# Up projection of a feed-forward layer: seven products of block sums in place of eight block products, for 8 of 22 tile pairs a layer

## The chip, the core and the metric

The kernel runs on one core of one Trainium2 chip. The metric is the device time of one execution in microseconds, the median of three runs. The core's engines work side by side: TensorE (PE in the profile; PEld is its weight load), VectorE (DVE), ScalarE (ACT), GpSimd (POOL) and SyncE (SP), whose queue issues the DMAs. They meet only in semaphores.

## The reference, cut to what matters

A model of two layers and one further block, on 512 tokens of width 1024, in float32. Each of the two layers ends with this feed-forward part (D_FF = 2816):

```python
h = rmsnorm(x, ffn_norm[l])
u = h @ ffn_w_up[l]                      # 1024 -> 2 * 2816
a, bv = u[..., :D_FF], u[..., D_FF:]
a = causal_dwconv(a, ffn_conv_w[l], ffn_conv_b[l])   # 3 taps along the tokens
x = x + (jax.nn.silu(a) * bv) @ ffn_w_down[l]
```

## The kernel before

Features lie on the 128 partitions, the 512 tokens along the free axis. Every float32 operand is kept as a high and a low part in the `F32R` type, and each product of blocks is three matmuls: high by high, high by low, low by high (`product`, lines 863 to 865). The high part of the weights is a ScalarE copy (`high`, line 1564), the low part a VectorE subtraction (`split_low`, line 1973); both work on a whole chunk of 2048 elements per partition (K = 8 blocks of 128 rows, 256 columns) or 1536 (K = 6). There are two slots of weights: chunk c lies in slot c % 2. SyncE loads chunk c once chunk c-2 is split (lines 1009 to 1018), ScalarE writes its high part once TensorE has finished chunk c-2, VectorE its low part after that.

The up projection has 22 tile pairs a layer. Pair f is one chunk: a gate tile and a value tile of 128 features each, 8 blocks by 3 matmuls of 512 columns, so 48 matmuls. The gate tile of an even f goes to PSUM bank 0, its value tile to bank 1, those of an odd f to banks 2 and 3. For each pair, in this order, VectorE scales the gate tile by the tokens' norm factor `rms_f` (line 2298), ScalarE takes the middle tap with the bias (line 1765), VectorE the other two taps (line 2303, twice), ScalarE the SiLU (line 1770), VectorE multiplies by `rms_f` again (line 2308) and by the value tile (line 2311), ScalarE and VectorE split the chunk that comes two pairs later, and then the hidden tile (lines 1775 and 2315). The 22 pairs are one loop of 11 iterations on VectorE, ScalarE and SyncE.

The down projection has 12 chunks in four groups of three (K = 8, 8, 6 blocks of the hidden axis); a group makes two output tiles of 512 tokens, one after the other within each chunk. VectorE adds each tile to `x_t` (line 2332), squares it and sums the squares (2334, 2338), writes the low part for the next stage (2341) and a second sum (2343). Its order is fixed: the split of two chunks, the group's two tiles, the split of the third chunk. After layer 0 the next layer begins with `raw_tiles` (lines 900 to 902), a norm statistic (803) and a gate product that needs VectorE's `kg` tile (2041). VectorE and ScalarE take their instructions strictly in program order, and almost every one is followed by a wait on its own semaphore. `upto` turns the count of an event into a threshold from loop registers.

## Time and profile before

| | |
|---|---|
| median of three runs | 2002.53 us (2002.37 to 2003.14) |
| the profiled execution | 2004.78 us, with a span of 2002.6 us from its first instruction to its last |
| TensorE busy | 1966.5 us, 98% of the span |
| VectorE busy | 1150.6 us, 57% |
| ScalarE busy | 826.2 us, 41% |
| mean granted TensorE clock | 0.995 |
| up projection of layer 0 | from about 263 to 506 us of the span |
| down projection of layer 0 | from about 506 to 626 us |

Busy time of TensorE counts from the first matmul of a queue to the modelled end of its last, and matmuls overlap: what one costs is read from the starts of two neighbours, not from its duration. Times in the rows below are microseconds from the start of the span, and means of groups are nanoseconds.

### The profile page before, as it was taken

Reading aid. Unit: us, or ns where it says so; the run is one execution under the profiler, and the core shown is the slowest. Engines: PE = TensorE matmul, PEld = TensorE weight load, DVE = VectorE, ACT = ScalarE, POOL = GpSimd, SP = SyncE. Lnnn points to the kernel's source line nnn. Section 1 sums busy time; section 2 is a strip of 40 time slices with the busy share of each in tenths; the row PEclk is TensorE's granted clock in tenths of the full one; section 3 lists DMA queues with packets and bytes.
Section 4 is the critical chain, followed back from the end, with each engine's and each line's share of the span. In section 5 each row is a group of like instructions: output and inputs, shape, how many; then the busy total and the mean of one; then the engine's idle time right before and its main releaser. Section 6 shows DMA issues by size and latency. Waiting matters only on the chain.

```text
span 2002.6 us, 29029 instructions
## 1 busy us (share of the span) xinstructions
PE 1966.5 (98%) x10962; PEld 1613.9 (81%) x10962; DVE 1150.6 (57%) x1382; ACT 826.2 (41%) x1211; POOL 25.9 (1%) x52
## 2 busy tenths in 40 slices
PE   7999999999999999999999999999999999999998
PEld 5897788888887897788888888987777766798888
DVE  6866765655445866766555445846664633443435
ACT  5445443333223345443333222334445555554444
POOL 2001000000000001000000000000000000000000
PEclk8999999999999999999999999999999999999999
DMA  6213133332224223133332223523332212232222
GB/s 192 75 47 105 43 105 105 84 105 85 94 95 120 69 55 106 43 105 96 93 104 85 95 95 80 183 73 99 89 110 68 63 53 64 84 115 76 92 87 85
DMA packets 239916, 181.26 MB, mean 91 GB/s; under 512 B 12842, under 2 KB 232232, under 8 KB 239422
## 3 DMA queue, kind: packets, MB, share of 16 engines
q1 hardware_dynamic: 237856, 177.37, 29.6%
q0 software_dynamic: 1520, 1.17, 0.3%
q10 hardware_dynamic: 430, 1.23, 0.3%
q8 instruction: 72, 1.18, 0.2%
q14 instruction: 38, 0.31, 0.1%
HBM read 168.21 MB, written 2.10 MB: 85 GB/s over the span
## 4 chain that ended last, share of the span: by engine, by line
PE 88%; DVE 6%; issue 2%; ACT 2%; DMA 1%; SPq 0%; DVEq 0%; ACTq 0%
PE ps L863 24%; PE ps L865 23%; PE ps L864 23%; PE ps L626 2%; PE ps L650 2%; PE ps L639 2%; DVE amat L2087 2%; PE ps L1285 1%; PE ps L1286 1%; PE ps L1287 1%; PE ps L506 1%; PE ps L475 1%; DMA w_raw<-in_w_in_dram 1%; PE ps L1169 1%; PE ps L495 1%
## 5 line engine op out<-in xcount | busy, mean ns | idle before, releaser
L863 PE MATMUL ps<-h_hi,w_hi 128*128 128x512 f32 x1376 | 553.8, 402 | 2.3 <-ACT qk L1557 2.0
L865 PE MATMUL ps<-h_hi,w_lo 128*128 128x512 f32 x1376 | 541.0, 393 | 0.0
L864 PE MATMUL ps<-h_lo,w_hi 128*128 128x512 f32 x1376 | 537.1, 390 | 0.0
L1973 DVE TENSOR_TENSOR w_lo<-w_raw,w_hi 128x2048 fp32r<-128x2048 f32 (+3 forms) x110 | 227.2, 2065 | 225.5 <-ACT w_hi L1564 218.0
L863 PEld LDWEIGHTS ps<-h_hi,w_hi 128*128 128x128 f32 x1376 | 259.4, 189 | 61.0 <-issue 7.4
L865 PEld LDWEIGHTS ps<-h_hi,w_lo 128*128 128x128 f32 x1376 | 259.2, 188 | 59.6
L864 PEld LDWEIGHTS ps<-h_lo,w_hi 128*128 128x128 f32 x1376 | 259.5, 189 | 56.0 <-issue 1.9
L1564 ACT ACTIVATE w_hi<-w_raw 128x2048 fp32r<-128x2048 f32 (+3 forms) x108 | 186.8, 1729 | 232.4 <-PE ps L865 211.9
L2362 DVE TENSOR_TENSOR w_lo<-w_raw,w_hi 128x1024 fp32r<-128x1024 f32 (+1 forms) x118 | 126.5, 1113 | 167.4 <-ACT w_hi L1816 166.7
L863 PE MATMUL ps<-w_hi,h_hi 128*128 128x256 f32 x544 | 152.4, 280 | 0.3 <-DVE h_lo L837 0.2
L864 PE MATMUL ps<-w_lo,h_hi 128*128 128x256 f32 x544 | 150.7, 277 | 0.0
L865 PE MATMUL ps<-w_hi,h_lo 128*128 128x256 f32 x544 | 150.7, 277 | 0.0
L863 PE MATMUL ps<-hid_hi,w_hi 128*128 128x512 f32 x352 | 138.7, 394 | 0.0
L865 PE MATMUL ps<-hid_hi,w_lo 128*128 128x512 f32 x352 | 138.0, 392 | 0.0
L864 PE MATMUL ps<-hid_lo,w_hi 128*128 128x512 f32 x352 | 136.6, 388 | 0.0
L1816 ACT ACTIVATE w_hi<-w_raw 128x1024 fp32r<-128x1024 f32 (+1 forms) x118 | 108.3, 965 | 4.1 <-issue 2.2
L863 PEld LDWEIGHTS ps<-w_hi,h_hi 128*128 128x128 f32 x544 | 102.3, 188 | 1.9 <-DVE h_lo L837 0.7
L1765 ACT ACTIVATE rms_a<-a_pad,g 128x512 f32<-128x512 f32 x44 | 35.9, 817 | 162.5 <-DVE a_pad L2298 162.5
L864 PEld LDWEIGHTS ps<-w_lo,h_hi 128*128 128x128 f32 x544 | 102.3, 188 | 0.1
L865 PEld LDWEIGHTS ps<-w_hi,h_lo 128*128 128x128 f32 x544 | 102.2, 188 | 0.0
L2303 DVE SCALAR_TENSOR_TENSOR rms_a<-a_pad,g,rms_a 128x512 f32<-128x512 f32 x88 | 66.2, 752 | 58.3 <-ACT rms_a L1765 51.7
L865 PEld LDWEIGHTS ps<-hid_hi,w_lo 128*128 128x128 f32 x352 | 66.1, 188 | 15.5
(390 smaller groups left out, 2767.6 us busy)
## 6 DMA issues: line engine op xcount, KB each, us to landing
w_raw<-in_ffn_w_up_dram SPq DMA_DIRECT2D x88, 512.0 KB, 4.6
w_raw<-in_w_in_dram SPq DMA_DIRECT2D x41, 1024.0 KB, 5.3
w_raw<-in_w_in_dram SPq DMA_DIRECT2D x32, 512.0 KB, 5.2
w_raw<-in_ffn_w_down_dram SPq DMA_DIRECT2D x32, 512.0 KB, 4.0
w_raw<-in_w_out_dram SPq DMA_DIRECT2D x12, 1024.0 KB, 5.6
w_raw<-in_ffn_w_down_dram SPq DMA_DIRECT2D x16, 384.0 KB, 3.4
swapped<-qk SPq DMA_DIRECT2D x96, 64.0 KB, 2.0
w_raw<-in_w_mem_kv_dram SPq DMA_DIRECT2D x4, 1024.0 KB, 5.8
```

Of the source, the lines that this page charges most:

```text
L626: ins = pe.matmul(ps[:, b, c:c + n], lhs, rhs, start=True, stop=True)
L639: ins = pe.transpose(ps[:, T_BANK + c // 512, c % 512:c % 512 + P], probs[:, e, c:c + P], ident)
L650: ins = pe.matmul(ps[64 * e:64 * e + 64, O_BANK, r * P:r * P + P], pairs[p].pv[e][k], probs_t[:, e, k * P:k * P + P], start=(k == 0), stop ...
L863: pe.matmul(dst, lh, rh, start=first and j == 0, stop=False)
L864: pe.matmul(dst, lh, rl, start=False, stop=False)
L865: ins = pe.matmul(dst, ll, rh, start=False, stop=last and j == len(order) - 1)
L1564: act.activation(w_hi[:, slot, 0:n], w_raw[:, slot, 0:n], ACT.Copy).then_inc(sem("w_high"), 1)
L1816: act.activation(w_hi[:, slot, q * n:q * n + n], w_raw[:, slot, q * n:q * n + n], ACT.Copy).then_inc(sem("w_high"), 1)
L1973: dve.tensor_tensor(w_lo[:, slot, 0:n], w_raw[:, slot, 0:n], w_hi[:, slot, 0:n].bitcast(F32), ALU.subtract).then_inc(sem("w_split"), 1)
L2087: dve.copy_predicated(amat[:].rearrange("p h t n -> p (h t) n"), levels[:, lv:lv + 1, :].to_broadcast([P, 4 * NT, P]), ps[:, MAIN:MAIN + 4 ...
L2303: dve.scalar_tensor_tensor(conv[:], a_pad[:, s, w:w + S], g[:, bass.ds(G_CONVW + w * KF + f, 1)], conv[:], ALU.mult, ALU.add).then_inc(sem ...
L2362: ins = dve.tensor_tensor(w_lo[:, slot, q * n:q * n + n], w_raw[:, slot, q * n:q * n + n], w_hi[:, slot, q * n:q * n + n].bitcast(F32), AL ...
```

## The change

In pairs 5, 7, ... 19 (8 of 22) the product of weights and tokens is taken as a 2 by 2 product of blocks: 4 of the 8 input blocks at a time by half of the tokens, gate rows and value rows. Seven products of block sums (Winograd's form of Strassen's scheme) take the place of eight: each is 4 blocks by 3 matmuls of 256 columns, so a pair has 84 matmuls of 256 columns in place of 48 of 512. The sums of tokens (`t_raw`) are made once a layer, during pairs 0 to 3. The sums of weights (`s_raw`) are made for each such pair by VectorE from the loaded chunk, and split like weights; one sum is written back into the chunk itself. VectorE puts the products together (`gate_fast`, `hidden_fast`). The hidden tiles stay unsplit in `hid` until pairs 20 and 21, where `hid_high` and `hid_low` split all 22. `rms_f` multiplies the down projection's output tiles in place of the SiLU's result. TensorE takes both output tiles of a down chunk block by block, so they are complete together. The counts of the new semaphores were added. The diff's core, its indentation taken back:

```diff
@@ constants and buffers @@
+FAST_FROM, FAST_TO = 5, 19
+FAST = (FAST_TO - FAST_FROM) // 2 + 1
-hid_hi, hid_lo = at("hid_hi", 0, [P, KF, S], F32R), at("hid_lo", 44, [P, KF, S], F32R)
+hid = at("hid", 0, [P, KF, S])
+hid_hi, hid_lo = at("hid_hi", 44, [P, KF, S], F32R), at("hid_lo", 0, [P, KF, S], F32R)
+y_blk = at("y_blk", 44, [P, 768])
+sums, u2 = at("sums", 40, [P, 3, 256]), at("u2", 43, [P, 256])
+s_raw, s_lo, s_hi = at("s_raw", 44, [P, 3, 4, P]), at("s_lo", 44, [P, 3, 4, P], F32R), at("s_hi", 50, [P, 3, 4, P], F32R)
+t_hi = at("t_hi", 56, [P, 4, 4, 256], F32R)
+t_raw, t_lo = at("t_raw", 72, [P, 4, 4, 256]), at("t_lo", 72, [P, 4, 4, 256], F32R)
...
@@ TensorE @@
+def fast_pair(i, n):
+    f = 2 * i + 1
+    t = T_UP + 2 * f
+    own = (slice(256, 512), slice(0, 256))
+    wh, wl = slot_view(w_hi, 1, KD), slot_view(w_lo, 1, KD)
+    block = lambda k0, row: lambda k: (wh[:, k0 + k, row * P:row * P + P], wl[:, k0 + k, row * P:row * P + P])
+    summed = lambda j: lambda k: (s_hi[:, j, k, :], s_lo[:, j, k, :])
+    tokens_ = lambda k0, c: lambda k: (h_hi[:, k0 + k, own[c]], h_lo[:, k0 + k, own[c]])
+    mixed_t = lambda j: lambda k: (t_hi[:, j, k, :], t_lo[:, j, k, :])
+    part = lambda bank, c: ps[:, bank, c * 256:c * 256 + 256]
+    split_ready(C_UP + f)
+    pe.wait_ge(sem("tile_copied"), upto(pe, "tile_copied", t - 2))
+    product(pe, part(5, 0), block(0, 1), tokens_(0, 0), range(4)).then_inc(sem("p1_done"), 1)
+    product(pe, part(2, 1), block(4, 1), tokens_(4, 0), range(4))
+    pe.wait_ge(sem("t_split"), upto(pe, "t_split", 4))
+    product(pe, part(4, 0), block(0, 0), mixed_t(2), range(4))
+    product(pe, part(4, 1), block(4, 0), mixed_t(3), range(4))
+    pe.wait_ge(sem("s_split"), upto(pe, "s_split", n + 1))
+    product(pe, part(3, 0), summed(1), mixed_t(1), range(4))
+    product(pe, part(3, 1), summed(0), mixed_t(0), range(4)).then_inc(sem("tile_done"), 1)
+    product(pe, part(2, 0), summed(2), tokens_(4, 1), range(4)).then_inc(sem("tile_done"), 1)
 up_tile(0, 0, 0)
 sum_stat(pe, 8)
-with pe.Fori(0, KF // 2 - 1) as i:
-    up_tile(i, 0, 1)
-    up_tile(i, 1, 0)
-    up_tile(i, 1, 1)
-    up_tile(i + 1, 0, 0)
-up_tile(KF // 2 - 1, 0, 1)
-up_tile(KF // 2 - 1, 1, 0)
-up_tile(KF // 2 - 1, 1, 1)
+up_tile(0, 0, 1)
+for f in range(1, FAST_FROM - 1):
+    for half in range(2):
+        up_tile(f // 2, f % 2, half)
+with pe.Fori(0, FAST) as n:
+    i = n + FAST_FROM // 2
+    for half in range(2):
+        up_tile(i, 0, half)
+    fast_pair(i, n)
+for f in range(FAST_TO + 1, KF):
+    for half in range(2):
+        up_tile(f // 2, f % 2, half)
 count["tile_done"] = 2 * C_DOWN
...
+            wh, wl = slot_view(w_hi, j % 2, K), slot_view(w_lo, j % 2, K)
+            if part == 0:
+                pe.wait_ge(sem("tile_copied"), upto(pe, "tile_copied", T_DOWN + 4 * i + 2 * q - 2))
+            for k in range(K):
+                pe.wait_ge(sem("hid_lo"), upto(pe, "hid_lo", 8 * part + k + 1))
+                for half in range(2):
+                    dst, c = ps[:, 2 * q + half, :], slice(half * P, half * P + P)
+                    h = 8 * part + k
+                    pe.matmul(dst, wh[:, k, c], hid_hi[:, h, :], start=h == 0, stop=False)
+                    pe.matmul(dst, wh[:, k, c], hid_lo[:, h, :], start=False, stop=False)
+                    ins = pe.matmul(dst, wl[:, k, c], hid_hi[:, h, :], start=False, stop=h == KF - 1)
+                    if k == K - 1:
+                        ins.then_inc(sem("tile_done"), tick("tile_done"))
@@ ScalarE @@
+def conv_start(f, slot):
+    act.wait_ge(sem("tile_copied"), upto(act, "tile_copied", T_UP + 2 * f + 1))
+    act.activation(conv[:], a_pad[:, slot, 2:S + 2], ACT.Identity,
+                   scale=g[:, bass.ds(G_CONVW + 2 * KF + f, 1)],
+                   bias=g[:, bass.ds(G_CONVB + f, 1)]).then_inc(sem("conv0"), 1)
+    act.wait_ge(sem("conv0"), upto(act, "conv0", f + 1))
+def conv_silu(f):
+    act.wait_ge(sem("conv"), upto(act, "conv", 2 * f + 2))
+    act.activation(conv[:], conv[:], ACT.Silu).then_inc(sem("silu"), 1)
+    act.wait_ge(sem("silu"), upto(act, "silu", f + 1))
+def up_high(f, slot):
+    act.wait_ge(sem("tile_done"), upto(act, "tile_done", T_UP + 2 * f + 2))
+    high(C_UP + f + 2, slot, KD, sum(dmas[slot][:C_UP // 2]) + f - slot + 4)
+def sums_high(f, n):
+    act.wait_ge(sem("s_sum"), upto(act, "s_sum", 4 * n + 4))
+    up_high(f, 1)
+    act.activation(s_hi[:], s_raw[:], ACT.Copy).then_inc(sem("s_high"), 1)
+def block_copies(j):
+    act.wait_ge(sem("t_sum"), upto(act, "t_sum", 4 * j))
+    act.activation(y_blk[:, 0:512], x_t[:, j], ACT.Copy, scale=col(G_FFN + j, 1))
+    act.activation(y_blk[:, 512:768], x_t[:, 4 + j, 256:512], ACT.Copy, scale=col(G_FFN + 4 + j, 1)).then_inc(
+        sem("y_blk"), tick("y_blk"))
+def block_high(j):
+    act.wait_ge(sem("t_sum"), upto(act, "t_sum", 4 * j + 4))
+    act.activation(t_hi[:, :, j, :], t_raw[:, :, j, :], ACT.Copy).then_inc(sem("t_high"), tick("t_high"))
+def hid_high(k):
+    act.wait_ge(sem("tile_copied"), upto(act, "tile_copied", T_UP + 2 * k + 2))
+    act.activation(hid_hi[:, k], hid[:, k], ACT.Copy).then_inc(sem("hid_hi"), 1)
+for f in range(FAST_FROM - 1):
+    conv_start(f, f % 2)
+    block_copies(f)
+    conv_silu(f)
+    if f + 2 < FAST_FROM:
+        up_high(f, f % 2)
+    else:
+        sums_high(f, 0)
+    block_high(f)
+def fast_act(n):
+    f = 2 * n + FAST_FROM - 1
+    conv_start(f, 0)
+    act.wait_ge(sem("p1_done"), upto(act, "p1_done", n + 1))
+    act.activation(sums[:, 2], ps[:, 5, 0:256], ACT.Copy).then_inc(sem("p1_kept"), 1)
+    up_high(f, 0)
+    conv_silu(f)
+    conv_start(f + 1, 1)
+    conv_silu(f + 1)
+with act.Fori(0, FAST - 1) as n:
+    fast_act(n)
+    sums_high(2 * n + FAST_FROM, n + 1)
+fast_act(FAST - 1)
+up_high(FAST_TO, 1)
+for f in (FAST_TO + 1, FAST_TO + 2):
+    conv_start(f, f % 2)
+    conv_silu(f)
+    up_high(f, f % 2)
+    for k in range(8 * (f - FAST_TO - 1), 8 * (f - FAST_TO)):
+        hid_high(k)
+for k in range(16, KF):
+    hid_high(k)
@@ VectorE @@
+def gate_fast(f, n):
+    pair = ps[:, 3:5, :].rearrange("p b n -> p (b n)")
+    dve.wait_ge(sem("tile_done"), upto(dve, "tile_done", T_UP + 2 * f + 1))
+    dve.wait_ge(sem("p1_kept"), upto(dve, "p1_kept", n + 1))
+    dve.tensor_tensor(u2[:], sums[:, 2], ps[:, 3, 0:256], ALU.add).then_inc(sem("fast_sum"), 1)
+    dve.wait_ge(sem("fast_sum"), upto(dve, "fast_sum", 3 * n + 1))
+    dve.tensor_tensor(sums[:, 0:2], u2[:].unsqueeze(1).to_broadcast([P, 2, 256]), halves(pair[:, 256:768]),
+                      ALU.add).then_inc(sem("fast_sum"), 1)
+    dve.wait_ge(sem("fast_sum"), upto(dve, "fast_sum", 3 * n + 2))
+    dve.tensor_tensor(halves(a_pad[:, 1, 2:S + 2]), sums[:, 0:2], halves(pair[:, 512:1024]),
+                      ALU.add).then_inc(sem("fast_sum"), 1)
+    dve.wait_ge(sem("fast_sum"), upto(dve, "fast_sum", 3 * n + 3))
+    dve.scalar_tensor_tensor(a_pad[:, 1, 2:S + 2], a_pad[:, 1, 2:S + 2], -1.0, rms_f[:], ALU.mult,
+                             ALU.mult).then_inc(sem("tile_copied"), 1)
+def conv_taps(f, slot):
+    dve.wait_ge(sem("conv0"), upto(dve, "conv0", f + 1))
+    for w in (1, 0):
+        dve.scalar_tensor_tensor(conv[:], a_pad[:, slot, w:w + S], g[:, bass.ds(G_CONVW + w * KF + f, 1)], conv[:],
+                                 ALU.mult, ALU.add).then_inc(sem("conv"), 1)
+        dve.wait_ge(sem("conv"), upto(dve, "conv", 2 * f + 2 - w))
+def hidden(f, src):
+    dve.wait_ge(sem("silu"), upto(dve, "silu", f + 1))
+    dve.wait_ge(sem("tile_done"), upto(dve, "tile_done", T_UP + 2 * f + 2))
+    dve.tensor_tensor(hid[:, bass.ds(f, 1), :].rearrange("p a n -> p (a n)"), src, conv[:],
+                      ALU.mult).then_inc(sem("tile_copied"), 1)
+    dve.wait_ge(sem("tile_copied"), upto(dve, "tile_copied", T_UP + 2 * f + 2))
+def hidden_fast(f, n):
+    dst = hid[:, bass.ds(f, 1), :].rearrange("p a n -> p (a n)")
+    dve.wait_ge(sem("tile_done"), upto(dve, "tile_done", T_UP + 2 * f + 2))
+    dve.tensor_tensor(halves(dst), sums[:, 0:3:2], halves(ps[:, 2, :]), ALU.add).then_inc(sem("c1_joined"), 1)
+    dve.wait_ge(sem("c1_joined"), upto(dve, "c1_joined", n + 1))
+    dve.wait_ge(sem("silu"), upto(dve, "silu", f + 1))
+    dve.tensor_tensor(dst, dst, conv[:], ALU.mult).then_inc(sem("tile_copied"), 1)
+    dve.wait_ge(sem("tile_copied"), upto(dve, "tile_copied", T_UP + 2 * f + 2))
+def plain(slot):
+    return ps[:, 2 * slot + 1, :]
+def weight_sums(f, n, first):
+    if first:
+        dve.wait_ge(sem("tile_done"), upto(dve, "tile_done", T_UP + 2 * f + 2))
+        dve.wait_ge(sem("w_loaded1"), upto(dve, "w_loaded1", 16 * (sum(n_dma[1::2][:C_UP // 2]) + f + 3)))
+        dve.tensor_tensor(s_raw[:, 0], raw1[:, 0:4, 0:P], raw1[:, 4:8, 0:P], ALU.add).then_inc(sem("s_sum"), 1)
+        dve.wait_ge(sem("s_sum"), upto(dve, "s_sum", 4 * n + 1))
+        dve.tensor_tensor(s_raw[:, 1], s_raw[:, 0], raw1[:, 0:4, P:2 * P], ALU.add).then_inc(sem("s_sum"), 1)
+        dve.wait_ge(sem("s_sum"), upto(dve, "s_sum", 4 * n + 2))
+    else:
+        dve.tensor_tensor(s_raw[:, 2], s_raw[:, 1], raw1[:, 4:8, P:2 * P], ALU.add).then_inc(sem("s_sum"), 1)
+        dve.tensor_tensor(raw1[:, 0:4, 0:P], raw1[:, 0:4, 0:P], raw1[:, 0:4, P:2 * P], ALU.add).then_inc(sem("s_sum"), 1)
+        dve.wait_ge(sem("s_sum"), upto(dve, "s_sum", 4 * n + 4))
+def sums_low(f, n):
+    split_low(C_UP + f + 2, 1, KD)
+    dve.wait_ge(sem("s_high"), upto(dve, "s_high", n + 1))
+    dve.tensor_tensor(s_lo[:], s_raw[:], s_hi[:].bitcast(F32), ALU.subtract).then_inc(sem("s_split"), 1)
+def block_sums(j):
+    y1, y2, y4 = y_blk[:, 256:512], y_blk[:, 0:256], y_blk[:, 512:768]
+    t = lambda q: t_raw[:, q, j, :]
+    dve.wait_ge(sem("y_blk"), upto(dve, "y_blk", j + 1))
+    dve.tensor_tensor(t(0), y1, y2, ALU.subtract).then_inc(sem("t_sum"), 1)
+    dve.scalar_tensor_tensor(t(2), x_t[:, 4 + j, 0:256], col(G_FFN + 4 + j, 1), y2, ALU.mult,
+                             ALU.subtract).then_inc(sem("t_sum"), 1)
+    dve.wait_ge(sem("t_sum"), upto(dve, "t_sum", 4 * j + 2))
+    dve.scalar_tensor_tensor(t(1), t(2), -1.0, y1, ALU.mult, ALU.subtract).then_inc(sem("t_sum"), 1)
+    dve.wait_ge(sem("t_sum"), upto(dve, "t_sum", 4 * j + 3))
+    dve.scalar_tensor_tensor(t(3), t(1), -1.0, y4, ALU.mult, ALU.subtract).then_inc(sem("t_sum"), 1)
+    dve.wait_ge(sem("t_sum"), upto(dve, "t_sum", 4 * j + 4))
+def block_low(j):
+    dve.wait_ge(sem("t_high"), upto(dve, "t_high", j + 1))
+    dve.tensor_tensor(t_lo[:, :, j, :], t_raw[:, :, j, :], t_hi[:, :, j, :].bitcast(F32), ALU.subtract).then_inc(
+        sem("t_split"), 1)
+def hid_low(k):
+    dve.wait_ge(sem("hid_hi"), upto(dve, "hid_hi", k + 1))
+    dve.tensor_tensor(hid_lo[:, k], hid[:, k], hid_hi[:, k].bitcast(F32), ALU.subtract).then_inc(sem("hid_lo"), 1)
+dve.wait_ge(sem("rms"), upto(dve, "rms", 4))
+dve.wait_ge(sem("pad"), upto(dve, "pad", 1))
+for f in range(FAST_FROM - 1):
+    gate_tile(f, f % 2)
+    conv_taps(f, f % 2)
+    hidden(f, plain(f % 2))
+    if f + 2 < FAST_FROM:
+        split_low(C_UP + f + 2, f % 2, KD)
+        block_sums(f)
+    else:
+        block_sums(f)
+        weight_sums(f, 0, True)
+        weight_sums(f, 0, False)
+        sums_low(f, 0)
+    block_low(f)
+def fast_even(n):
+    f = 2 * n + FAST_FROM - 1
+    gate_tile(f, 0)
+    conv_taps(f, 0)
+    split_low(C_UP + f + 2, 0, KD)
+    hidden(f, plain(0))
+with dve.Fori(0, FAST - 1) as n:
+    fast_even(n)
+    f = 2 * n + FAST_FROM
+    gate_fast(f, n)
+    weight_sums(f, n + 1, True)
+    conv_taps(f, 1)
+    weight_sums(f, n + 1, False)
+    hidden_fast(f, n)
+    sums_low(f, n + 1)
+fast_even(FAST - 1)
+gate_fast(FAST_TO, FAST - 1)
+conv_taps(FAST_TO, 1)
+hidden_fast(FAST_TO, FAST - 1)
+split_low(C_UP + FAST_TO + 2, 1, KD)
+for f in (FAST_TO + 1, FAST_TO + 2):
+    gate_tile(f, f % 2)
+    conv_taps(f, f % 2)
+    hidden(f, plain(f % 2))
+    split_low(C_UP + f + 2, f % 2, KD)
+    for k in range(8 * (f - FAST_TO - 1), 8 * (f - FAST_TO)):
+        hid_low(k)
+for k in range(16, KF):
+    hid_low(k)
...
-            dve.tensor_tensor(one(x_t), one(x_t), ps[:, j, :], ALU.add).then_inc(sem("tile_copied"), 1)
+            dve.tensor_tensor(b_sb[:], ps[:, j, :], rms_f[:], ALU.mult).then_inc(sem("down_scaled"), 1)
+            dve.wait_ge(sem("down_scaled"), upto(dve, "down_scaled", m + 1))
+            dve.tensor_tensor(one(x_t), one(x_t), b_sb[:], ALU.add).then_inc(sem("tile_copied"), 1)
```

## Rows read from the trace of the kernel before

**Rows 1.** Busy in a stretch: PE, PEld, DVE, ACT, POOL (instructions), clock, DMA
```profile
400.00:500.00 100.00, 100.00 (x439) 82.04 (x438) 58.97 (x65) 34.95 (x36) 0.00 (x0) 1.00 0.33 95
```

**Rows 2.** Timeline, TensorE: start, duration; every twelfth matmul, three places
```profile
400.10 0.39 PE L863 MATMUL ps<-h_hi,w_hi 128*128 128x512 f32 x1
402.85 0.39 PE L863 MATMUL ps<-h_hi,w_hi 128*128 128x512 f32 x1
...
1952.56 0.28 PE L1540 MATMUL ps<-w_hi,h_hi 128*128 128x256 f32 x1
1953.97 0.28 PE L1540 MATMUL ps<-w_hi,h_hi 128*128 128x256 f32 x1
...
1963.26 0.28 PE L1540 MATMUL ps<-w_hi,h_hi 128*128 128x256 f32 x1
1964.62 0.28 PE L863 MATMUL ps<-w_hi,h_hi 128*128 128x256 f32 x1
```

**Rows 3.** Timeline of VectorE, one pair
```profile
401.17 0.69 DVE L2298 TENSOR_TENSOR a_pad<-ps,rms_f 128x512 f32<-128x512 f32 x1 [0.61 <-PE ps L865]
403.01 0.75 DVE L2303 SCALAR_TENSOR_TENSOR rms_a<-a_pad,g,rms_a 128x512 f32<-128x512 f32 x1 [1.15 <-ACT rms_a L1765]
403.92 0.75 DVE L2303 SCALAR_TENSOR_TENSOR rms_a<-a_pad,g,rms_a 128x512 f32<-128x512 f32 x1 [0.15 <-DVE rms_a L2303]
408.75 2.29 DVE L1973 TENSOR_TENSOR w_lo<-w_raw,w_hi 128x2048 fp32r<-128x2048 f32 x1 [1.58 <-ACT w_hi L1564]
410.96 0.68 DVE L2315 TENSOR_TENSOR hid_lo<-b_sb,hid_hi 128x512 f32 x1
```

**Rows 4.** Timeline of ScalarE, the same pair
```profile
402.05 0.82 ACT L1765 ACTIVATE rms_a<-a_pad,g 128x512 f32<-128x512 f32 x1 [3.99 <-DVE a_pad L2298]
404.76 0.63 ACT L1770 ACTIVATE rms_a<-rms_a 128x512 f32<-128x512 f32 x1 [1.90 <-DVE rms_a L2303]
406.64 1.92 ACT L1564 ACTIVATE w_hi<-w_raw 128x2048 fp32r<-128x2048 f32 x1 [1.25 <-PE ps L865]
```

**Rows 5.** Groups by line and shape, VectorE and ScalarE, other widths
```profile
L2535 DVE TENSOR_TENSOR y_tok<-ps,g_row 128x256 f32<-128x256 f32 x16 | 6.8, 424 | 15.1 <-ACT sq L1947 14.9
L1973 DVE TENSOR_TENSOR w_lo<-w_raw,w_hi 128x1536 fp32r<-128x1536 f32 x8 | 14.1, 1759 | 48.3 <-ACT w_hi L1564 48.3
...
L1614 ACT ACTIVATE sig_r<-tm 128x1024 f32<-128x1024 f32 x2 | 2.1, 1061 | 0.1
L1947 ACT ACTIVATE sq<-ps 128x256 f32<-128x256 f32 x16 | 6.1, 382 | 21.9 <-PE ps L865 18.8 <-PE ps L1542 3.0
```

**Rows 6.** Timelines of VectorE and ScalarE, start of the up projection
```profile
270.65 0.69 DVE L2298 TENSOR_TENSOR a_pad<-ps,rms_f 128x512 f32<-128x512 f32 x1 [1.23 <-ACT rms_f L810]
291.33 0.69 DVE L2298 TENSOR_TENSOR a_pad<-ps,rms_f 128x512 f32<-128x512 f32 x1 [0.64 <-PE ps L865]
...
272.10 0.82 ACT L1765 ACTIVATE rms_a<-a_pad,g 128x512 f32<-128x512 f32 x1
275.80 1.92 ACT L1564 ACTIVATE w_hi<-w_raw 128x2048 fp32r<-128x2048 f32 x1 [0.33 <-ACT rms_a L1770]
```

**Rows 7.** Timeline of VectorE, second tile of a down group, next split
```profile
596.30 0.69 DVE L2332 TENSOR_TENSOR x_t<-x_t,ps 128x512 f32 x1 [0.29 <-DVE rms_f L2343]
600.43 2.29 DVE L1973 TENSOR_TENSOR w_lo<-w_raw,w_hi 128x2048 fp32r<-128x2048 f32 x1 [0.27 <-DVE rms_f L2343]
```

**Rows 8.** Timelines of VectorE and TensorE, layer 0 to layer 1
```profile
630.79 2.29 DVE L1973 TENSOR_TENSOR w_lo<-w_raw,w_hi 128x2048 fp32r<-128x2048 f32 x1 [0.27 <-DVE rms_f L2343]
640.69 0.69 DVE L2041 TENSOR_TENSOR kg<-ps,rms_a 80x512 f32<-80x512 f32 x1 [0.60 <-DVE cq L2041]
...
637.95 0.48 PE L863 MATMUL ps<-h_hi,w_hi 128*128 128x512 f32 x1
```

**Rows 9.** A long wait of TensorE's; busy times in a stretch behind it
```profile
PE ps L639 <- ACT prob_bt L697: 4.4, 4, 2.0
...
1622.00:1624.00 2.00, 2.00 (x6) 1.52 (x6) 0.65 (x1) 1.56 (x4) 0.00 (x0) 0.50 0.56 165
```

67 lines of the change are left out of this document (11 added, 56 removed).

## The prediction, blind

> **What bounds the kernel now.** I read the page's busy shares first (in the table of times), then the windows, then the timeline of each engine over one pair. In the up projection TensorE never rests: 100 us busy of 100, at full clock, beside 59 us of VectorE and 35 us of ScalarE [rows 1]. It starts one matmul of 512 columns every 0.229 us (twelve in 2.75 us) [rows 2], so a pair is 48 x 0.229 = 10.99 us and two pairs 21.97. Nothing but TensorE's work sets the time there. VectorE waits for it before each gate tile (0.61 us in the bracket) and for ScalarE in between, 0.15 to 1.6 us at a time [rows 3]. So the question is what a fast pair saves TensorE, and whether the two other engines, which take their instructions in order, can follow.
>
> **TensorE's part.** A fast pair is 7 products x 4 blocks x 3 = 84 matmuls of 256 columns. Twelve of them take 1.41 us in one place and 1.36 in another [rows 2]: 0.1175 or 0.1133 each, so 9.87 or 9.52 us a pair. I take 0.116, as the first place lies directly behind a stream of 512 columns, as here: 9.74 us, 1.24 less than 10.99. Sixteen such pairs would give 19.9 us, if nothing else came to bound them (17.9 to 23.5).
>
> **The loop of an even and a fast pair.** TensorE would need 10.99 + 9.74 = 20.7 us. Now follow VectorE and ScalarE through one iteration, from `u2` to the next `u2`. Durations: VectorE 0.69 us for 512 elements, 0.75 with a scalar from memory, 2.29 for a chunk [rows 3]; ScalarE 0.82, 0.63, 1.92 [rows 4]; VectorE 0.42 for 256 and 1.76 for 1536, ScalarE 0.38 for 256 [rows 5]. Hand-overs: VectorE to ScalarE 0.19 (401.86 to 402.05), ScalarE's chunk to VectorE's 0.19 (408.56 to 408.75), tap to tap 0.15, and an overlap of 0.08 where nothing is waited for (411.04 to 410.96) [rows 3, 4]. A wait on the engine's own last result is not shown alone. Its bounds are -0.08, the overlap, and 0.33, SiLU to chunk, where two more thresholds stand behind it [rows 6]. I take 0.04, and 0.3 where more thresholds follow, as a tile of the down projection has five instructions of 3.57 us in 4.13, of which the last gap is 0.27 [rows 7].
> - The gate put together, 0.42 + 3 x 0.69 + three gaps: 2.6 us. First two weight sums: 3.9. Gap and two taps, 0.29 + 1.65: 5.9. Second two sums: 7.2.
> - ScalarE's high part, 0.38 + 1.92: 9.5. VectorE's low part, 0.19 + 2.29: 12.0. Here the chunk of the next fast pair is ready.
> - `s_lo` and the next gate tile, 1.76 + 0.69 less overlaps: 14.3. ScalarE's middle tap, its copy of the first product and the even chunk's high part, 0.19 + 0.82 + 0.17 + 0.38 + 1.84: 17.7. Low part and hidden tile: 20.8. Gap: 21.1.
>
> ScalarE's high part must wait for the second weight sums, which write into the chunk, and these stand behind the taps; the hidden tile stands behind the low part. So this is one chain of 21.1 us, and it is longer than TensorE's 20.7. The saving is 21.97 - 21.1 = 0.9 us an iteration, not 1.24. The Trainium skill speaks against this ("VectorE: DVE Perf Modes", The DRAIN you can't avoid): a semaphore after each instruction costs nothing extra, which would leave the chain below TensorE's time and the whole at the 1996 us of the first rival; the rows' 0.15 behind an own wait, against an overlap without one, do not bear it out. Whether a matmul of 256 columns costs 0.113 or 0.1175 us changes nothing, as 20.9 is below 21.1 too.
>
> **Before the loop.** In pairs 0 to 3 VectorE and ScalarE make and split the sums of tokens. One pair's chain: gate 0.69, 0.19, middle tap 0.82, 0.14, taps 1.6, 0.09, SiLU 0.63, 0.33, high 1.92, 0.19, low 2.29, four sums of 256 elements 1.7, then ScalarE's high part of 1024 elements 1.06 [rows 5] and VectorE's low part 1.2 (between 0.69 and 1.76) with gaps of 0.1: 13.0 us, against 10.99 of TensorE. The removed `rms_f` product lies beside ScalarE's chunk and gives nothing. The first gate tile starts at 270.65 and its middle tap 0.57 us late (272.10), so that of pair 3 starts at 270.65 + 0.57 + 3 x 13.0 = 310.2 [rows 6]. From there to the end of chunk 5's split are gate to SiLU 4.2, hidden 0.8, token sums 1.7, four weight sums 2.8, high 2.2, low 2.5: 324.4. TensorE ends pair 4 two and a half pairs after the gate tile of 291.33: 318.7 [rows 6]. **TensorE waits 5.7 us before the first fast pair.** The next one comes 22.3 us later (s_lo, t_lo and an even pair stand before its `u2`), then six at 21.1: 148.9 us, against 7 x 21.97 = 153.8 before: 4.9 less. The last fast pair is 1.24 shorter. The up projection nets 5.7 - 4.9 - 1.2 = -0.4 us a layer.
>
> A wait this long may drop the clock: behind a wait of up to 2.0 us (at 1618 us) a stretch ran at 0.50, the lower level of 1.2 GHz [rows 9]. That would stretch fast pair 5 by 1.7 us, but 20.7 + 1.7 is just what the chain needs there (22.3), so I count nothing; at most 2 us a layer.
>
> **Behind the loop.** In pairs 20 and 21 the splits of 16 hidden tiles are put between: 8 x 0.61 us on ScalarE, 8 x 0.65 on VectorE each. Pair 21's work then ends about 11 us behind its tiles, but TensorE is on the first down chunk, which needs hidden tiles 0 to 7 alone; tile 8's low part comes about 0.3 us late. Each down tile has one product more, 0.73 us, and both tiles of a group end together, so VectorE's work on the first is no longer beside the second. It starts 0.6 us before the group ends, takes 2 x (4.13 + 0.73) = 9.7, then a split of 2.29: ready 11.4 us behind the group, where TensorE wants it after 10.99 [rows 3, 7]. That is 0.5 us, three times a layer. The down projection: +1.8 us a layer. Before, that split began 4.13 us behind the second tile's start [rows 7] and had room.
>
> **Layer 0 to 1.** The split of 630.79 ends at 633.1 and `kg` at 641.38, just as TensorE, which begins its tile at 637.95 and needs `kg` after 15 matmuls, comes to 641.4 [rows 8]. With the split ending at 637.4 and the same 4.35 us of small work behind it (0.5 to 1 us a piece), `kg` is ready at 643.9: +2.5 us, once. Behind layer 1 nothing waits for it.
>
> **Sum.** 2 x (-0.4 + 1.8) + 2.5 = +5.3; with the rounding of the terms +5. The sum is made against the profiled execution, whose 2004.78 us are its span of 2002.6 and 2.2 around it; it stands 2.2 above the median of 2002.53. I carry the difference over to the median: 2007.5 us.
>
> **Rivals.** A measurement of this kernel can tell 0.2%, 4.0 us, from no change.
> - *The waits are nearly free* (faster). If own waits cost as little as the overlap of 0.08 suggests, the chain loses some 0.9 us and falls below 20.7: TensorE sets the loop again. Then a layer is +4.1 before the loop, -8.2 in it, -1.2, +0.9: -4.4; twice, with +2.2: 1996. For: the 0.04 within a tile. Against: 0.15 and 0.27 in loops of the same kind [rows 3, 7]. It decides at 0.4 us of gaps an iteration. By the Trainium skill's sentence above it would be so. Chance 0.22.
> - *Between the two*, 1998.5 to 2003. Chance 0.10.
> - *Longer gaps* (slower). The new thresholds are computed from loop registers, up to four to a step. With 0.3 at each own wait the chain is 21.9, no gain in the loop; 7.4 us are waited for before it and 3.5 lost behind it: (7.4 + 0.6 - 1.2 + 3.5) x 2 + 3.5 = +24. Half of that excess is 2017. Chance 0.13.
> - *The forecast*, 2003 to 2014, chance 0.55, of which 0.25 lies within 0.2%.
>
> That the change doesn't do what it says, I exclude but for the cadence, which is bounded above. Sum: faster 0.22, same 0.35, slower 0.43. The range of 1995 to 2017 leaves a tenth out on either side; the forecast's own is 2003 to 2014.
>
> **What would show it.** Right: TensorE idle some 6 us before the first matmul of 256 columns on `ps` in either layer, released by `w_lo`; idle 0.2 to 0.6 us before each later fast pair, released by `w_lo` too; fast pairs 21.0 to 21.2 us apart; 0.5 us before each down group's second chunk; the `kg` tile 2 to 3 us late. Wrong: fast pairs 20.7 apart without idle time (the first rival), or 21.9 (the third); a first wait under 3 us, which would mean that the chain of pairs 0 to 3 is below 12.3.

## The result, and the profile after

The changed kernel takes 2007.78 us (median of seven runs, 2006.70 to 2011.83), the kernel before 2003.14 us beside it (seven runs, 2002.37 to 2006.12): a ratio of 1.0025, 95% interval 1.0015 to 1.0034. So it is 4.6 us slower, on a forecast of 2007.5. The profiled execution has a span of 2004.8 us, that of the kernel before 2002.6. A fast pair below is one of the eight that are made from block sums, an even pair one of the ordinary ones between them.

TensorE does less work and the kernel is not faster. The page's busy shares and clock:

```profile
PE 1956.7 (98%) x11538; PEld 1630.8 (81%) x11538; DVE 1257.8 (63%) x1538; ACT 867.6 (43%) x1267; POOL 25.9 (1%) x52
...
PEclk8999999999999999999999999999999999999999
```

VectorE has 107 us more work than before, ScalarE 41. The waits of TensorE (line, releaser: us in total, times, longest) have three rows of more than a microsecond that the kernel before has not:

```profile
PE ps L872 <- DVE w_lo L2068: 7.8, 2, 3.9
...
PE ps L1396 <- DVE w_lo L2068: 2.0, 6, 0.4
...
PE ps L1190 <- DVE kg L2136: 1.7, 1, 1.7
```

The first stands before the first fast pair of each layer (line 872 is `product`), the second before the second chunk of three of the four down groups, the third at the start of layer 1. TensorE's timeline over the first fast pair's start, the fast pair after it, and the start of the next, then the first fast pair of layer 1:

```profile
321.60 0.38 PE L872 MATMUL ps<-h_hi,w_hi 128*128 128x256 f32 x1 [3.92 <-DVE w_lo L2068]
...
344.21 0.28 PE L872 MATMUL ps<-h_hi,w_hi 128*128 128x256 f32 x1
...
345.62 0.28 PE L872 MATMUL ps<-h_hi,w_hi 128*128 128x256 f32 x1
...
351.29 0.28 PE L872 MATMUL ps<-t_hi,s_hi 128*128 128x256 f32 x1
...
352.73 0.28 PE L872 MATMUL ps<-h_hi,s_hi 128*128 128x256 f32 x1
...
354.17 0.39 PE L872 MATMUL ps<-h_hi,w_hi 128*128 128x512 f32 x1
...
365.17 0.28 PE L872 MATMUL ps<-h_hi,w_hi 128*128 128x256 f32 x1
...
928.74 0.58 PE L872 MATMUL ps<-h_hi,w_hi 128*128 128x256 f32 x1 [3.92 <-DVE w_lo L2068]
```

In the loop TensorE waits for nothing. A fast pair takes 354.17 - 344.21 = 9.96 us, an even pair 11.00, so fast pairs are 20.96 us apart against 21.97 for two pairs before. Twelve matmuls of the first product take 1.41 us, 0.1175 each; twelve of a product with summed weights take 1.44, 0.120 each. And the first fast pair is followed by the next only after 22.61 us, 1.65 more than the others, and in layer 1 only after 23.42 us (928.74 to 952.16), 2.46 more. Busy times in two stretches (window: its length, then PE, PEld, DVE, ACT and POOL busy with their instructions, granted clock, DMA share, GB/s) show why:

```profile
321.60:326.40 4.80, 4.80 (x27) 4.80 (x28) 3.63 (x4) 1.25 (x3) 0.00 (x0) 0.65 0.76 213
...
644.50:651.20 6.70, 6.70 (x17) 5.15 (x17) 5.22 (x6) 3.88 (x7) 0.00 (x0) 0.54 0.61 194
```

Behind the wait of 3.92 us much of the stretch ran at the lower level of the clock, 1.2 GHz, with matmuls of 256 columns 0.213 us apart (in layer 1 the first 24 of them). The same happened behind the wait for `kg`, where matmuls of 512 columns are 0.425 us apart until 650.8. TensorE's timeline there:

```profile
637.05 0.48 PE L872 MATMUL ps<-h_hi,w_hi 128*128 128x512 f32 x1
...
643.25 1.52 PE L1190 MATMUL ps<-kg,wg 16*128 16x512 f32 x2 [1.73 <-DVE kg L2136]
...
660.73 1.17 PE L1151 MATMUL ps<-lin 32*128 32x128 f32 x32
```

And in the kernel before:

```profile
642.36 1.12 PE L1181 MATMUL ps<-kg,wg 16*128 16x512 f32 x2
656.67 1.17 PE L1142 MATMUL ps<-lin 32*128 32x128 f32 x32
```

The kernel before takes 656.67 - 637.95 = 18.72 us for this stretch (its first matmul is in [rows 8]), the changed one 660.73 - 637.05 = 23.68: 4.96 us more, of which 1.79 stand ahead of the `kg` matmul and 3.17 behind it. I call it the `kg` stretch. The feed-forward parts that the change touches are even: from the up projection's first value tile to the end of the layer, layer 0 takes 369.39 us against 369.42, layer 1 369.75 against 369.79. Within each, gains and costs cancel. TensorE's matmuls at the first value tile and at the start of the down projection, layer 0, of the kernel before and then of the changed one:

```profile
268.53 0.80 PE L863 MATMUL ps<-h_hi,w_hi 128*128 128x512 f32 x1
...
505.16 0.39 PE L863 MATMUL ps<-hid_hi,w_hi 128*128 128x512 f32 x1
...
267.66 0.80 PE L872 MATMUL ps<-h_hi,w_hi 128*128 128x512 f32 x1
...
501.79 0.39 PE L1396 MATMUL ps<-hid_hi,w_hi 128*128 128x512 f32 x1
```

So the up projection takes 234.13 us instead of 236.63 (234.74 in layer 1), 2.50 and 1.89 less, with the waits before the first fast pairs and the slow clock behind them included. The down projection takes 122.47 instead of 120.62, 1.85 more in either layer, and what follows it 0.62 more in layer 0.

So the parts that the change touches lose 4.96 - 0.03 - 0.04 = 4.9 us, all of it in one stretch of 24 us. The two profiled executions are only 2.2 us apart, because the changed kernel's was 2.7 us faster in parts that are the same in both kernels: 0.9 ahead of the up projection, 0.3 in layer 1 ahead of its up projection, and 1.5 behind layer 1, where the kernel before ran a stretch at half clock [rows 9] and the changed one did not. That is chance, so the 4.6 us between the medians and the 4.9 us of the traces agree no better than within a few microseconds.

### The profile page after: what moved, and what is told of

Its sections match the earlier page's. It is cut to its first block, busy times and chain, and to the rows that moved or that the text cites. A ratio compares the mean times of both kernels' runs of the same rounds, so it can differ in the third digit from the quotient of the medians.

```text
span 2004.8 us, 30593 instructions
## 1 busy us (share of the span) xinstructions
PE 1956.7 (98%) x11538; PEld 1630.8 (81%) x11538; DVE 1257.8 (63%) x1538; ACT 867.6 (43%) x1267; POOL 25.9 (1%) x52
## 4 chain that ended last, share of the span: by engine, by line
PE 79%; DVE 12%; ACT 4%; issue 4%; DVEq 0%; DMA 0%; ACTq 0%; SPq 0%
PE ps L872 18%; PE ps L874 17%; PE ps L873 17%; PE ps L1396 3%; PE ps L1397 3%; PE ps L1398 3%; PE ps L635 2%; PE ps L659 2%; PE ps L648 2%; DVE w_lo L2068 2%; DVE amat L2182 2%; PE ps L1294 1%; PE ps L1295 1%; PE ps L1296 1%; PE ps L515 1%
## 5 line engine op out<-in xcount | busy, mean ns | idle before, releaser
L872 PE MATMUL ps<-h_hi,w_hi 128*128 128x512 f32 (+1 forms) x1248 | 489.6, 392 | 10.2 <-DVE w_lo L2068 7.8
L874 PE MATMUL ps<-h_hi,w_lo 128*128 128x512 f32 (+1 forms) x1248 | 478.9, 384 | 0.0
L873 PE MATMUL ps<-h_lo,w_hi 128*128 128x512 f32 (+1 forms) x1248 | 476.8, 382 | 0.0
L872 PEld LDWEIGHTS ps<-h_hi,w_hi 128*128 128x128 f32 x1248 | 237.2, 190 | 63.6 <-issue 17.5
L874 PEld LDWEIGHTS ps<-h_hi,w_lo 128*128 128x128 f32 x1248 | 237.2, 190 | 46.7
L873 PEld LDWEIGHTS ps<-h_lo,w_hi 128*128 128x128 f32 x1248 | 237.4, 190 | 45.1 <-issue 1.9
L1396 PEld LDWEIGHTS ps<-hid_hi,w_hi 128*128 128x128 f32 x352 | 66.1, 188 | 19.4 <-DVE w_lo L2068 3.0
```

The lines of the kernel that those rows point to most:

```text
L872: pe.matmul(dst, lh, rh, start=first and j == 0, stop=False)
L873: pe.matmul(dst, lh, rl, start=False, stop=False)
L874: ins = pe.matmul(dst, ll, rh, start=False, stop=last and j == len(order) - 1)
L1396: pe.matmul(dst, wh[:, k, c], hid_hi[:, h, :], start=h == 0, stop=False)
```

## The experiments

Times are medians; ratios are against the kernel before, run beside them. Its own medians were 2004.36 us beside sums_early, down_halves, amat_late and both, 2004.42 beside plain, plain_halves, extra_op and s_from_w, 2005.73 beside both_swapped and 2004.19 beside the last two, and 2003.14 beside the changed kernel. So differences of a microsecond or two between kernels of different groups are not read from the times but from the traces.

| run | us | ratio, 95% interval |
|---|---|---|
| sums_early | 1993.41 | 0.9945 (0.9931 to 0.9959) |
| down_halves | 2000.50 | 0.9977 (0.9966 to 0.9987) |
| amat_late | 2002.27 | 0.9991 (0.9982 to 1.0000) |
| both | 1987.45 | 0.9910 (0.9895 to 0.9925) |
| plain | 2011.72 | 1.0036 (1.0023 to 1.0050) |
| plain_halves | 2002.95 | 0.9994 (0.9985 to 1.0003) |
| extra_op | 2020.93 | one run |
| s_from_w | 2006.35 | one run |
| both_swapped | 1987.76 | 0.9915 (0.9902 to 0.9929) |
| extra_reordered | 2011.78 | one run |
| both_reordered | 1983.98 | 0.9898 (0.9882 to 0.9915) |

**Which wait costs what.** In the changed kernel, VectorE's timeline over pair 1, one of the four in which the token sums are made:

```profile
282.84 0.68 DVE L2391 TENSOR_TENSOR a_pad<-ps,rms_f 128x512 f32<-128x512 f32 x1
...
288.90 2.29 DVE L2068 TENSOR_TENSOR w_lo<-w_raw,w_hi 128x2048 fp32r<-128x2048 f32 x1 [1.41 <-ACT w_hi L1607]
...
294.04 1.23 DVE L2468 TENSOR_TENSOR t_lo<-t_raw,t_hi 128x1024 fp32r<-128x1024 f32 x1 [1.20 <-ACT t_hi L1833]
295.18 0.68 DVE L2391 TENSOR_TENSOR a_pad<-ps,rms_f 128x512 f32<-128x512 f32 x1
```

A pair's chain is 295.18 - 282.84 = 12.34 us, and 2.6 of them are two idle times: 1.41 for ScalarE's high part of the chunk, 1.20 for its high part of the token sums. The sums could be made in the first of these. That is the edit of sums_early:

```diff
-y_blk = at("y_blk", 44, [P, 768])
+y_blk = at("y_blk", 40, [P, 768])
...
     if f + 2 < FAST_FROM:
+        block_sums(f)
         split_low(C_UP + f + 2, f % 2, KD)
-        block_sums(f)
     else:
-        block_sums(f)
         weight_sums(f, 0, True)
         weight_sums(f, 0, False)
+        block_sums(f)
         sums_low(f, 0)
```

> Only the order of VectorE's steps in pairs 0 to 3 is changed: the token sums stand ahead of the chunk's low part, in the time in which VectorE waits for ScalarE's high part (1.41 us a pair), and in pair 3 the weight sums stand ahead of the token sums; the scratch of the scaled tokens lies in another place. My theory: TensorE sets the loop (20.96 us an iteration), and the wait of 3.92 us before the first fast pair, with the 1.65 us that the half clock costs behind it, adds straight to the time, twice. One pair's chain falls from 12.35 us to about 10.3, below TensorE's 10.99, so both go: 2 x 5.57 = 11.1 us less, near 1996.7 us. Rival, from my prediction: the chain of VectorE and ScalarE is what sets the loop, and a first fast pair that comes earlier only waits later, before each of the next ones: 0 to 3 us less, 2005 to 2008 us.

Measured: 1993.41 us, 14.4 less than the changed kernel (15.6 if each is taken against the kernel before beside it). VectorE over the same pair, then the first two fast pairs on TensorE:

```profile
285.94 0.42 DVE L2457 TENSOR_TENSOR t_raw<-y_blk 128x256 f32<-128x256 f32 x1
...
287.80 2.29 DVE L2068 TENSOR_TENSOR w_lo<-w_raw,w_hi 128x2048 fp32r<-128x2048 f32 x1
290.01 1.22 DVE L2468 TENSOR_TENSOR t_lo<-t_raw,t_hi 128x1024 fp32r<-128x1024 f32 x1
291.15 0.69 DVE L2391 TENSOR_TENSOR a_pad<-ps,rms_f 128x512 f32<-128x512 f32 x1
...
317.97 0.28 PE L872 MATMUL ps<-h_hi,w_hi 128*128 128x256 f32 x1
...
338.96 0.28 PE L872 MATMUL ps<-h_hi,w_hi 128*128 128x256 f32 x1
```

Both idle times are gone, there is no wait before the first fast pair, and the next follows after 20.99 us, at full clock. From the up projection's first value tile to the end of the layer it is 363.59 us in layer 0, 5.8 less, and 363.40 in layer 1, 6.35 less, where the clock had cost more. The `kg` stretch is 1.9 us shorter as well, though nothing there was edited: TensorE waited 1.37 us instead of 1.73, and from `kg` to the end of the stretch it is 15.91 us instead of 17.48 (14.31 before). The wait and what it does to the clock were real time; the rival, that the loop would swallow it, is out. My 11.1 us were too few: I had 1.65 us for the clock in both layers and nothing for the `kg` stretch.

The edit of down_halves, in the down projection's loop on TensorE (the matmuls are as they were):

```diff
-for k in range(K):
+last = part == 2
+for step in ([(half, k) for half in range(2) for k in range(K)] if last else [(None, k) for k in range(K)]):
+    k = step[1]
     pe.wait_ge(sem("hid_lo"), upto(pe, "hid_lo", 8 * part + k + 1))
-    for half in range(2):
+    for half in (range(2) if step[0] is None else [step[0]]):
```

> Only the last of a down group's three chunks is changed: half after half again instead of block by block, so the first tile of a group ends 4.1 us ahead of the second. My theory: the group's split is ready some 8 us behind the group instead of 11.3, so the six waits of 0.33 us go (2.0 us), kg in layer 1 is not late (1.7 us), and the clock does not fall to its lower level behind it (some 3.1 us over sixteen matmuls): 6.8 us less, near 2001.0 us. Rival: the waits come from the product with rms_f added to each tile, which stays: then kg is still over a microsecond late and the clock drops all the same, and only 0 to 2 us are won, 2006 to 2008 us.

Measured: 2000.50 us, 7.3 less. The six waits are gone, the down projection takes 120.62 us as in the kernel before, and the wait for `kg` is 0.4 us, with the clock up behind it (14.31 us to the end of the stretch, as before). And amat_late:

```diff
-dve.memset(amat[:], 0.0).then_inc(sem("amat0"), tick("amat0"))
-dve.wait_ge(sem("amat0"), upto(dve, "amat0"))
 dve.wait_ge(sem("tile_done"), upto(dve, "tile_done", 2))
 evict(0, cq[:, 4])
 evict(1, kg[0:80, :])
+dve.memset(amat[:], 0.0).then_inc(sem("amat0"), tick("amat0"))
+dve.wait_ge(sem("amat0"), upto(dve, "amat0"))
```

> Only the clearing of amat (1.76 us on VectorE) at a layer's start is moved behind the tile of kg; the down projection stays as it is. My theory: VectorE is then ready for the tile ahead of kg when ScalarE's factor is, so kg is not late (1.7 us) and the clock stays up behind it (3.1 us): 4.8 us less, near 2003.0 us; the six waits of 0.33 us in the down projections stay. Rival: the clock's fall at 644 us is no consequence of this wait, and only the 1.7 us go: 2006.1 us; or the clearing is late for its own reader, and nothing is won.

Measured: 2002.27 us, 5.5 less. TensorE no longer waits for `kg`, and the stretch from 636.25 to 654.97 takes 18.72 us, exactly that of the kernel before. The six waits stay (2.0 us). So the 4.96 us hung on a tile with no room left: either edit saves them, an earlier end of the down projection's last split, or one clearing of 1.76 us out of the way. Then early sums and the halves' order together:

> The order of VectorE's steps in pairs 0 to 3 as in the run with early sums, and the last chunk of each down group half after half. My theory: the two are independent and TensorE sets everything between, so the gains add: 11.1 + 6.8 = 17.9 us less than the changed kernel, near 1990 us, 13 us (0.65%) less than the kernel before; that is the 16 us by which TensorE's work is shorter, less what two fast pairs' worth of slower matmuls take. Rival, the loop bound by VectorE and ScalarE: 1999 to 2003 us.

Measured: 1987.45 us, a ratio of 0.9910. Neither the waits at the fast pairs nor those in the down projection nor `kg` are in its list of waits. The up projection takes 228.59 us, 8.04 less than in the kernel before, and 228.57 in layer 1.

**The change without its fast pairs.** In plain, all 22 pairs are eight block products (the loops of the three engines run ordinary pairs, with no sums); plain_halves adds the edit of down_halves:

```diff
-fast_pair(i, n)
+for half in range(2):
+    up_tile(i, 1, half)
```

> All 22 pairs are computed as eight block products again (no token sums, no weight sums, no fast pairs); the rest of the change stays: the norm factor behind the down projection, the hidden tiles split into parts at the end, the down projection block by block. My theory: what is left is what the rest of the change costs beside the kernel before: six waits of 0.33 us in the down projections (2.0 us) and kg late in layer 1 with the clock's fall behind it (5.0 us): 7 us more than the kernel before, near 2010 us. Rival: kg is late in the changed kernel because of the fast pairs, and the rest of the change alone costs 2 us or nothing.

> As the run with eight block products everywhere, and the last chunk of each down group half after half. My theory: both costs of the rest of the change are gone, so it runs as the kernel before, near 2003 us (within 0.1%), which leaves the 16 us between it and the run with both mendings to the fast pairs alone. Rival: the product with rms_f and the late splits of the hidden tiles still cost 2 us or more.

Measured: 2011.72 us, 7.3 above the kernel before beside it, and 2002.95, level with it. TensorE's waits in plain:

```profile
PE ps L1397 <- DVE w_lo L2065: 2.0, 6, 0.4
...
PE ps L1190 <- DVE kg L2133: 1.7, 1, 1.7
```

They are those of the changed kernel to a tenth. So with the last chunk half after half the product with `rms_f` and the late splits cost nothing that shows; what is lost behind the loop hangs on the down projection's order. And the fast pairs alone are worth 2002.95 - 1987.45 = 15.5 us by the times, and 2 x 8.04 = 16.1 by the traces, as plain_halves has the up projection at 236.63 us, like the kernel before.

**What bounds the loop.** VectorE over one iteration of the changed kernel, from `u2` (`u` in the profile) to the next:

```profile
353.07 0.42 DVE L2397 TENSOR_TENSOR u<-sums,ps 128x256 f32<-128x256 f32 x1 [0.49 <-PE ps L874]
...
354.97 0.69 DVE L2405 SCALAR_TENSOR_TENSOR a_pad<-a_pad,rms_f 128x512 f32<-128x512 f32 x1
...
359.57 0.68 DVE L2445 TENSOR_TENSOR w_raw<-w_raw 128x512 f32<-128x512 f32 x1
...
362.56 2.29 DVE L2068 TENSOR_TENSOR w_lo<-w_raw,w_hi 128x2048 fp32r<-128x2048 f32 x1 [0.75 <-ACT w_hi L1607]
...
366.44 0.68 DVE L2391 TENSOR_TENSOR a_pad<-ps,rms_f 128x512 f32<-128x512 f32 x1
...
372.86 0.68 DVE L2418 TENSOR_TENSOR hid<-ps,rms_a 128x512 f32 x1
374.03 0.42 DVE L2397 TENSOR_TENSOR u<-sums,ps 128x256 f32<-128x256 f32 x1 [0.48 <-PE ps L874]
```

`u2` waits for TensorE, and the chunk of the next fast pair is ready at 364.85, 0.32 us before TensorE starts on it (365.17). How much room is that? The extra step of extra_op:

```diff
 gate_fast(f, n)
+dve.tensor_tensor(b_sb[:], rms_f[:], rms_f[:], ALU.mult).then_inc(sem("fast_sum"), 1)
+dve.wait_ge(sem("fast_sum"), upto(dve, "fast_sum", 4 * n + 4))
 weight_sums(f, n + 1, True)
```

> The changed kernel with one more product of 512 elements on VectorE, with a wait on its own result, behind the put-together gate of each fast pair but the last: some 0.8 us more in VectorE's chain of an iteration. My theory: TensorE sets the loop at 20.96 us and VectorE's chain is some 20.6 us by itself, as VectorE waits 0.49 us for TensorE before u2 and TensorE's next chunk is ready 0.3 us early. Then an iteration grows to about 21.4 us (0.5 of the 0.8), with TensorE idle some 0.4 us before each fast pair, released by w_lo. Rival, my prediction's chain: it was at its bound already, so the distance grows by the whole 0.8 to 21.8. Third: if there is over 0.8 us of room, nothing changes.

TensorE at the starts of two fast pairs, the chunk between, and the next `u2`:

```profile
345.55 0.38 PE L872 MATMUL ps<-h_hi,w_hi 128*128 128x256 f32 x1 [0.73 <-DVE w_lo L2068]
...
365.02 2.29 DVE L2068 TENSOR_TENSOR w_lo<-w_raw,w_hi 128x2048 fp32r<-128x2048 f32 x1 [0.74 <-ACT w_hi L1607]
...
367.51 0.38 PE L872 MATMUL ps<-h_hi,w_hi 128*128 128x256 f32 x1 [0.73 <-DVE w_lo L2068]
...
376.46 0.42 DVE L2397 TENSOR_TENSOR u<-sums,ps 128x256 f32<-128x256 f32 x1 [0.46 <-PE ps L874]
```

They are 21.96 us apart: the extra 1.02 us (with its gap, from the distance of `u2` and `w_lo`: 12.80 us against 11.78) came through but for 0.02, where I had expected half of it. My reading of the room was wrong, because `u2` waits for TensorE and TensorE waits for what `u2` begins. That is a loop of its own through three engines: six products of the fast pair to `u2` (365.17 to 374.03, 8.86 us), `u2` to the end of the low part (11.78), and 0.20 to TensorE (367.31 to 367.51 in this run). Its sum is 20.84 us, 0.12 below TensorE's 20.96. With 1.02 for the extra step and 0.10 by which the first matmul behind a wait starts the next one later (8.95 us from there to `u2` here), it is the 21.96 measured, to 0.02. The next run keeps the extra step and takes work out of that loop, while the chain of VectorE and ScalarE keeps all its steps:

```diff
 weight_sums(f, n + 1, True)
+weight_sums(f, n + 1, False)
 conv_taps(f, 1)
-weight_sums(f, n + 1, False)
+split_low(C_UP + f + 2, 1, KD)
 hidden_fast(f, n)
-sums_low(f, n + 1)
+summed_low(n + 1)
```

On ScalarE the chunk's high part goes ahead of SiLU accordingly; `summed_low` is `sums_low` without the chunk.

> The run with one more product in VectorE's chain showed fast pairs 21.95 us apart instead of 21.4: almost the whole 1.0 us came through. My theory now: the loop that binds goes through three engines, from the first matmul of a fast pair over six products (8.9 us) to u2, and from u2 over sums, taps, ScalarE's high part and VectorE's low part (11.8 us, 12.8 with the extra step) to the next fast pair. In the changed kernel it is 20.84 us, 0.12 below TensorE's own 20.96. This kernel keeps the extra step, but puts both pairs of weight sums ahead of the taps, ScalarE's high part ahead of SiLU, and the low part ahead of the hidden tile. Then u2 to low part is 10.9 us and this loop 20.0, so fast pairs are 20.96 to 21.1 us apart and TensorE's idle time of 0.73 us before each is gone but for 0.1; the time is near the changed kernel's. Rival, the chain of my prediction: VectorE and ScalarE between themselves are the bound; their steps are all still there, so the distance stays at 21.6 to 21.95.

VectorE's `u2` twice, and TensorE at the fast pair between:

```profile
354.44 0.42 DVE L2401 TENSOR_TENSOR u<-sums,ps 128x256 f32<-128x256 f32 x1 [0.33 <-DVE hid L2422]
...
366.67 0.39 PE L872 MATMUL ps<-h_hi,w_hi 128*128 128x256 f32 x1 [0.23 <-DVE hid L2432]
...
375.89 0.42 DVE L2401 TENSOR_TENSOR u<-sums,ps 128x256 f32<-128x256 f32 x1 [0.33 <-DVE hid L2422]
```

Fast pairs are 21.45 us apart: neither number. What sets the pace now is the chain of my prediction: VectorE no longer waits for TensorE before `u2`, only 0.33 us behind its own hidden tile. TensorE still has idle time before a fast pair, but it waits for the hidden tile of the fast pair before (`hid`, 0.2 us) and not for the chunk. 21.45 us are that chain with 1.02 us too much and 0.37 us less idle time before the low part (0.38 instead of 0.75). Without both it is 21.45 - 1.02 + 0.37 = 20.80 us. So 0.37 of the 0.5 us won were the chain's own. That the three-engine loop had set the pace of extra_op, and not this chain, shows in extra_op's trace, by a narrow margin: there `u2` waited 0.46 us for TensorE, against the 0.33 that it needs behind its own hidden tile. In the changed kernel three loops therefore lie within 0.16 us, the first two worked out from these rows: 20.80, 20.84 and TensorE's 20.96.

**The distance of matmuls of 256 columns.** In s_from_w the products with summed weights read `w_hi` and `w_lo` instead, so those pairs leave out the block sums of weights that they should use:

```diff
-summed = lambda j: lambda k: (s_hi[:, j, k, :], s_lo[:, j, k, :])
+summed = lambda j: block(4 * (j % 2), j // 2)
```

> The changed kernel, but the three products of a fast pair with summed weights take blocks of w_hi and w_lo as their stationary operand in place of s_hi and s_lo, so those pairs do not compute the reference's hidden tiles; everything else, the making of s_hi and s_lo too, stays. In the changed kernel these 36 matmuls start 0.120 us apart, and the 48 others 0.1175 (in two pairs 0.1133). My theory: the stationary operand's buffer makes the difference, so all 84 start 0.1175 or 0.1133 apart here and a fast pair takes 9.87 or 9.52 us. Rival: it is their place in the pair (the banks that they write, what VectorE and ScalarE do meanwhile), and the 36 stay at 0.120.

TensorE over two fast pairs of this run, each from its first matmul to that of the even pair behind it:

```profile
365.52 0.29 PE L872 MATMUL ps<-h_hi,w_hi 128*128 128x256 f32 x1
...
375.07 0.39 PE L872 MATMUL ps<-h_hi,w_hi 128*128 128x512 f32 x1
...
407.25 0.29 PE L872 MATMUL ps<-h_hi,w_hi 128*128 128x256 f32 x1
...
417.16 0.40 PE L872 MATMUL ps<-h_hi,w_hi 128*128 128x512 f32 x1
```

9.55 us and 9.91, 0.1137 and 0.118 over all 84: the 0.120 belongs to the summed stationary operand. Is it where that lies?

```diff
-s_raw, s_lo, s_hi = at("s_raw", 44, ...), at("s_lo", 44, ...), at("s_hi", 50, ...)
-t_hi, t_raw, t_lo = at("t_hi", 56, ...), at("t_raw", 72, ...), at("t_lo", 72, ...)
+s_raw, s_lo, s_hi = at("s_raw", 76, ...), at("s_lo", 76, ...), at("s_hi", 82, ...)
+t_hi, t_raw, t_lo = at("t_hi", 44, ...), at("t_raw", 60, ...), at("t_lo", 60, ...)
```

> The kernel with both mendings, with the places of two buffers exchanged: the summed weights (s_hi, s_lo) stand behind the token sums (t_hi, t_lo) in the on-chip memory, 32 KB higher than before. The run that took w_hi and w_lo as stationary operands showed 0.1175 us a matmul for all 84, so the buffer of the stationary operand makes the 0.120. Theory one: it is the buffer's address, and at its new place the summed products start 0.1175 or 0.1133 apart: a fast pair takes 9.87 us instead of 9.97, and 0.1 us an iteration are won, 1.5 us in all, 1986 us (by the profile's distances rather than by the time, as that is less than a median can tell). Theory two: it is how the operand is laid out or which engines wrote it, whatever its address: 0.120 stays, and the time stays at 1987.5 us. A side result is whether t_hi and t_lo, moved too, change the 0.1175 of products three and four.

Measured: 1987.76 us, and the 36 matmuls stay at 0.120. Not this address, then; the layout (256 columns a block in `w_hi`, 128 in `s_hi`) was not tried. The last run takes the order of extra_reordered into the kernel of the run both, without the extra step:

> The kernel with both mendings, with the steps of a fast pair in the loop in the order of the run above (all weight sums ahead of the taps, high part ahead of SiLU, low part ahead of the hidden tile). My theory: TensorE's 10.99 + 9.97 = 20.96 us set the loop already, so the 1.9 us by which the chunk is ready earlier are room and no time: 1987.5 us, within a microsecond, fast pairs 20.96 us apart, and 20.75 where a fast pair falls to 0.1133 a matmul. Rival: there is idle time in that loop that the trace does not show, and 1 to 2 us go; or SiLU, which now stands behind the high part, makes the hidden tile late, and the time rises.

Measured: 1983.98 us, 3.5 less than both, which I had not expected. TensorE over one fast pair of it:

```profile
359.91 0.28 PE L872 MATMUL ps<-h_hi,w_hi 128*128 128x256 f32 x1
...
361.27 0.28 PE L872 MATMUL ps<-h_hi,w_hi 128*128 128x256 f32 x1
...
366.79 0.28 PE L872 MATMUL ps<-t_hi,s_hi 128*128 128x256 f32 x1
368.23 0.28 PE L872 MATMUL ps<-h_hi,s_hi 128*128 128x256 f32 x1
369.67 0.39 PE L872 MATMUL ps<-h_hi,w_hi 128*128 128x512 f32 x1
```

Twelve matmuls of the first product take 1.36 us, 0.1133 each, in 14 of the 16 fast pairs (all but each layer's first); a fast pair takes 9.76 us and fast pairs are 20.75 apart. 14 x 0.21 is 2.9 of the 3.5 us. It is the fastest kernel here, 1.0% below the kernel before.

## Why the prediction came out right

The time was met, 2007.8 on 2007.5, and the ratio is in the outcome that had the most chance (slower by over 0.2%, though its interval reaches 0.15%). But that is partly luck: terms were off in both directions. The up projection came out 2.50 and 1.89 us faster where I had 0.4 a layer, and the passage from layer 0 to 1 2.5 us slower than I had it.

- **The loop's saving: right in size, wrong in its bound.** I had 0.9 us an iteration from a chain of 21.1 us. It is 1.0, and TensorE sets it. The chain is 20.80 us. By its steps: the chunk ready after 11.78 us (12.0), the next gate tile done at 14.05 (14.3), the hidden tile at 20.47 (20.8), then the 0.33 that I had as 0.3. Most of the 0.3 us too many are two hand-overs at the fast pair's chunk: VectorE's fourth sum to ScalarE's high part took 0.27 where I had 0.38, and ScalarE's end to VectorE's low part 0.12 where rows 3 and 4 have 0.19.
- **The step that failed for the rivals' weights**: "it decides at 0.4 us of gaps". The gaps were smaller, though by 0.3 and not 0.4, and TensorE's time was longer, so the loop came out as the first rival had it (TensorE bound), while the time did not. I had 0.116 us a matmul and 9.74 a pair, where it is 0.1186 and 9.96: 36 of the 84 matmuls have a sum of weights as their stationary operand, and no matmul in [rows 2] has. The upper bound of 0.1175 was too low. So TensorE's own time was 20.96 and not 20.7, and passed the chain's from the other side: errors of 0.2 and 0.3 us that left the saving at 1.0.
- **What I left out**: the loop through three engines, 20.84 us. I followed `u2` to `u2` over VectorE and ScalarE and took TensorE's products as given. It changed nothing here, but would have bound first had the chain been a bit longer, as extra_op shows.
- **Before the loop.** Forecast 5.7 us, measured 3.92, since a pair's chain is 12.34 instead of 13.0, three times. These pairs are not in a loop over pairs, and there the hand-overs between VectorE and ScalarE took 0.03 to 0.04 us (283.52 to 283.56, 284.38 to 284.41, 285.95 to 285.99), where I had 0.19, 0.14 and 0.09 from pairs in a loop; SiLU to chunk took 0.18 for 0.33. With 1.8 us in each layer this is the largest error of the forecast.
- **The clock behind it.** I counted nothing, "as the chain needs it there". It cost 1.65 us in layer 0 and 2.46 in layer 1, as the next fast pair came so much later. The chain needed nothing there: VectorE waited 0.87 us for TensorE before the first `u2`, and in sums_early, without the wait, the next fast pair came after 20.99 us. The bound of 2 us a layer held in layer 0 and not in layer 1.
- **The down projection.** Forecast 0.5 us three times a layer, and start to start it is 0.49, 0.55 and 0.48 (0.72, 0.78 and 0.71 less the 0.229 of a matmul), though the list of waits has only 0.30 to 0.39 of each; the matmul behind each wait adds 0.1. The down projection is 1.85 us longer, forecast 1.8. `hid_lo` was never late (0.3 forecast). Right, and so was the first half of its reason, by down_halves: the tiles' order alone takes the waits away. Whether they would come without the added product, no run shows.
- **Layer 0 to 1.** Forecast +2.5 us, measured +4.96: 1.79 for `kg`, and 3.17 for the clock that fell behind it. I had read in rows 9 what a wait of 2 us can do, applied it to the fast pair and not to this wait.
- **The sum.** Up projection -2.50 and -1.89 us measured, -0.4 a layer forecast; down projection +1.85 against +1.8, with another 0.62 behind that of layer 0 that I did not have. So a layer is -0.03 and -0.04 against +1.4, and the passage +4.96 against +2.5: 4.9 against 5.3. Errors of 2.9 us in the layers and 2.5 in the passage nearly cancelled.
- **The rule of the Trainium skill** ("VectorE: DVE Perf Modes", The DRAIN you can't avoid) is that a semaphore behind each instruction costs nothing extra. The trace agrees for the semaphore alone: an instruction that raises one and is not waited for leaves the overlap of 0.08 us (the gate's last step ends at 355.66, the next starts at 355.58). It is the wait that costs: a plain wait on the last result leaves 0.03 us (353.49 to the next start at 353.52), so some 0.1 us. Where loop-computed thresholds, another semaphore or an operand indexed by the loop follow, it is 0.15 to 0.33. So waits on own results cost what I had put in (0.04 and 0.3). The forecast's use of the rule, that it might leave the chain below TensorE's time, came true for other reasons, the shorter hand-overs between engines and TensorE's own longer time; that the time would be 1996 us did not, as the waits outside the loop took the gain.

What stays open: why the summed stationary operand costs 0.120, and why 0.1133 and 0.1175 alternate.

## What to carry to other kernels

Before a change that gives TensorE's work to other engines, list every place where they hand something to TensorE with less than a microsecond of room, outside the loop too: here the 15.5 us that the fast pairs are worth were lost at nine such waits and to the clock behind three of them, and all won back by changing the order of steps, with no work removed. Price a wait of one or two microseconds at more than its length: behind it TensorE may run at half clock for a while. And follow a loop once through all engines that it passes, the one thought to be the bound among them.

## What the runs showed of the hardware

- **A wait's price in clock varies.** TensorE waits 1.97 us for `prob_bt` in both kernels: in the kernel before the granted clock was down behind it [rows 9], and from there to the next `prob_bt` matmul it took 4.91 us (1620.40 to 1625.31); in the changed kernel the clock was 1.00 from 1624 to 1630 and the same took 3.32 (1624.15 to 1627.47). Behind the wait for `kg` the clock cost 3.2 us after 1.73 us of waiting, 3.4 after 2.27 (extra_op), 1.7 after 1.61 (extra_reordered), 1.6 after 1.37 (sums_early) and nothing after 0.4. Behind the waits of 3.92 us at a first fast pair it fell in all six kernels that have them, ten times for 1.6 us and twice for 2.5.
- **Distances of matmuls of 256 columns**: 0.1133, 0.1175 and 0.120 us at full clock, 0.213 at the lower level. By the Trainium skill ("TensorE: Matmul & The Clock Gate", Wait — 56ns, not 53.3ns?) it is N over 2.4 GHz and 2.5 ns, by which an estimate for 256 is 0.109 us; no stream here was as fast, and here every matmul has a weight load of its own (11538 of each). At 1.2 GHz it is N over the clock by that section, 0.213, and the trace agrees.
- **When the pair is released may matter.** In both_reordered the last thing that a fast pair waits for, a hidden tile, ended 0.9 us ahead of it (the chunk's low part 2.2), and its first four products ran at 0.1133 in 14 of 14 pairs. In the changed kernel, sums_early, down_halves, amat_late, both and both_swapped the low part ended 0.3 us ahead, and 74 of 84 such pairs ran at some 0.1175, the others (three in the changed kernel) at 0.1133 in all or most of the four products, with the same 0.3 us. In extra_reordered, where the low part ended 1.4 us ahead but TensorE waited for the hidden tile, none ran at 0.1133. The first fast pair of a layer is an exception (0.1175 with 2.6 us), but there the split of the token sums is still going on as it starts. This is a coincidence with one order of steps, not a cause shown. By the Trainium skill ("TensorE: Matmul & The Clock Gate", the table at its head) the engine's queue pulls weight loads ahead of matmuls in flight; whether this is that, no run shows.
- **Hand-overs between VectorE and ScalarE**: the first three of a pair took 0.03 to 0.04 us in pairs 0 to 3 of the changed kernel, which are not in a loop over pairs, and 0.14 to 0.19 for even pairs in the loop. From ScalarE's high part to VectorE's low part it was 0.19 in both. No run changes the loop alone, so the cause is not shown.
